# The second head's softmax division in block 1's attention: from VectorE to ScalarE

## The chip, the cores and the metric

The kernel is one program on one core of a Trainium2 chip. The metric is device time in microseconds (us) of one execution. Engines are named as in the profile: PE is TensorE's matmul, PEld its weight load, DVE is VectorE, ACT ScalarE, POOL GpSimd, SP the engine that issues most DMAs.

## What is computed

Two transformer blocks, each of two layers, on 256 tokens (block 1 also on 256 context tokens) with a model width of 1024. The part that matters here is the attention of block 1. It has two branches of eight heads of 64: a neighbourhood attention with a relative bias, and a window attention whose softmax has a sink. Each query looks at its own sequence and at the context:

```python
def sink_softmax(s, sink):
    m = jnp.maximum(jnp.max(s, axis=-1, keepdims=True), sink)
    e = jnp.exp(s - m)
    return e / (jnp.sum(e, axis=-1, keepdims=True) + jnp.exp(sink - m))

s = jnp.concatenate([s_w, s_c], axis=-1)        # scores: own tokens, context
p = jax.nn.softmax(s, axis=-1)                  # neighbourhood; window: sink_softmax
o = p[own] @ v + p[context] @ v_ctx
```

In layer 0 the context tokens are updated too, so they also ask (they look at the context alone); in layer 1 they don't.

## The kernel before

The kernel streams 1 MB chunks of weights through a ring, splits each into a high and a low part (ScalarE line 245, VectorE line 259) and multiplies with three matmuls per product (lines 301 to 303). That takes nearly all of the span. Between two such stretches, in each layer of block 1, stands `attend_both` (line 1738), which runs both branches as one loop of steps with the class `Attention`.

A step is one pair of heads and one tile of 128 queries. The 512 keys (256 own, 256 context) are looked at by tiles of own tokens; tiles of context tokens look at 256 keys. Layer 0 has 32 steps, in which steps of 512 keys and of 256 keys alternate (tiles 0, 2, 1, 3 for each of 8 pairs of heads). Layer 1 has 16 steps, all of 512 keys. Two neighbouring steps of layer 0, the first of 512 keys, are called a pair of steps below.

The order of the work on each engine is written out by hand, one iteration t after the other, and the engines meet through semaphores:

- TensorE: scores of step t (line 808); transposes of the probabilities of step t-2 (`pe_turns`, line 829, eight of 128x128 for 512 keys, four for 256); products with the values of step t-3 (line 843).
- VectorE: adds the bias to both heads' scores of step t and takes the maxima (line 864); reciprocal of the sums of step t-1 (line 873); negated maximum of step t (lines 879, 882); multiplies both heads' probabilities of step t-1 by the reciprocal (line 889); at the end of a pair of heads copies the output (line 902); then in some iterations one or two taps of block 1's convolution (lines 1520, 1524), work that is spread over the loop.
- ScalarE: copies the transposed probabilities of step t-2 from PSUM (`act_turned`, line 914), then the two exponentials of step t, one per head, each with its sum (`act_exp`, line 929).

The waits around the division:

```python
pe.wait_ge(scaled.sem, self.at(scaled, v))                    # line 824, transposes of v
if v:
    pe.wait_ge(turned_sb.sem, self.at(turned_sb, v - 1))      # line 826
dve.wait_ge(small.sem, self.at(small, v))                     # line 886
for half in range(2):                                         # line 887
    p = self.prob[:, v % self.PROBS, half, 0:n]
    o = dve.tensor_scalar(p, p, self.fac[:, v % 3, half:half + 1], ...)
o.then_inc(scaled.sem, 1)
```

`prob` has three buffers, `probT` two, the score banks two. Block 2 uses the same class (lines 2029 and 2039), with an order of its own around it.

Of the kernel before, what the change touches and what calls it, by code (L numbers as in the profile page):

```python
# [23 lines left out]
ACT = mybir.ActivationFunctionType  # L24
# [5 lines left out]
S = 256  # L30
# [87 lines left out]
def build(nc, wstream, xT, ctxT, cT, consts, vecs, rpb, rel, out):  # L118
    ctx = ExitStack()
    with ctx:  # L120
# [8 lines left out]
        def count(name):  # L129
            return Count(ctx.enter_context(nc.semaphore(name)))  # L130
# [594 lines left out]
        small = count("small")  # L725
        floored = count("floored")
        scaled = count("scaled")
        turned = count("turned")
        turned_sb = count("turned_sb")
        summed = count("summed")  # L730
# [3 lines left out]
        class Attention:  # L734
# [7 lines left out]
            LAG_T, LAG_V, PROBS, TURNS = 2, 3, 3, 2  # L742

            def __init__(self, steps, dst, bufs, turn_bank=None, outs=(3072, 3584), halves=False, stacked=False,
                         first_set=0):
                self.stacked, self.first_set = stacked, first_set
                self.steps, self.dst, self.U = steps, dst, len(steps)
                self.turn_bank, self.outs, self.halves = turn_bank, outs, halves
                self.SETS = 1 if turn_bank and not stacked else 2
                self.prob, self.probT, self.mx, self.den, self.fac, self.neg = bufs  # L750
                self.base = {c: c.n for c in (scored, biased, sunk, shift, exped, small, scaled, turned,
                                              turned_sb, summed, taken, taken_hi, floored)}
                self.nsunk = np.cumsum([int("sink" in u) for u in steps]).tolist()
                self.nfloor = np.cumsum([int("floor" in u) for u in steps]).tolist()
                pairs = [u["pair"] for u in steps]
                self.ends = [n for n in range(self.U) if n == self.U - 1 or pairs[n + 1] != pairs[n]]
                for c in (scored, shift, exped, small, scaled, turned, turned_sb, summed):
                    c.n += self.U
                biased.n += 2 * self.U
                sunk.n += self.nsunk[-1]  # L760
                floored.n += self.nfloor[-1]
                taken.n += len(self.ends)
                taken_hi.n += len(self.ends) if halves else 0
                self.length = self.U + self.LAG_V + 1
# [57 lines left out]
            def pe_turns(self, pe, v):  # L822
                if 0 <= v < self.U:
                    pe.wait_ge(scaled.sem, self.at(scaled, v))
                    if v:
                        pe.wait_ge(turned_sb.sem, self.at(turned_sb, v - 1))
                    for half in range(2):
                        for a, w in self.blocks(v):
                            mm = pe.transpose(self.turn(v, half, a)[0:w],  # L829
                                              self.prob[:, v % self.PROBS, half, a:a + w], const("ident"))  # L830
                    mm.then_inc(turned.sem, 1)
# [16 lines left out]
            def dve(self, dve, t):  # L848
                v = t - 1
                if t < self.U:  # L850
                    u = self.steps[t]
                    n = u["n"]
                    slot = t % self.PROBS
                    if t >= self.PROBS:
                        dve.wait_ge(turned.sem, self.at(turned, t - self.PROBS))
                    if "sink" in u:
                        dve.tensor_copy(self.prob[:, slot, :, n:n + 1], u["sink"].unsqueeze(2)).then_inc(sunk.sem, 1)
                    dve.wait_ge(scored.sem, self.at(scored, t))
                    for half in range(2):
                        o, s_in = self.prob[:, slot, half, 0:n], self.score(t, half, n)  # L860
                        if n > 256:
                            o = o.rearrange("p (a k) -> p a k", k=256)
                            s_in = s_in.rearrange("p (a k) -> p a k", k=256)
                        dve.tensor_tensor_reduce(o, s_in, u["bias"][half], 1.0, -3e38, ALU.add, ALU.max,  # L864
                                                 self.mx[:, t % 3, half:half + 1]).then_inc(biased.sem, 1)
                if 0 <= v < self.U:
                    u = self.steps[v]
                    dve.wait_ge(exped.sem, self.at(exped, v))
                    d, f = self.den[:, v % 3, :], self.fac[:, v % 3, :]
                    if "floor" in u:  # L870
                        dve.tensor_scalar(d, d, 1e-30, None, ALU.max).then_inc(floored.sem, 1)
                        dve.wait_ge(floored.sem, self.base[floored] + self.nfloor[v])
                    dve.reciprocal(f, d).then_inc(small.sem, 1)
                if t < self.U:
                    u = self.steps[t]
                    dve.wait_ge(biased.sem, self.base[biased] + 2 * t + 2)
                    m, g = self.mx[:, t % 3, :], self.neg[:, t % 3, :]
                    if "sink" in u:
                        dve.scalar_tensor_tensor(out=g, in0=m, scalar=-1.0, in1=u["minus_sink"], op0=ALU.mult,
                                                 op1=ALU.min).then_inc(shift.sem, 1)  # L880
                    else:
                        dve.tensor_scalar(g, m, u.get("floor", -3e38), -1.0, ALU.max, ALU.mult  # L882
                                          ).then_inc(shift.sem, 1)
                if 0 <= v < self.U:
                    n, gate = self.steps[v]["n"], self.steps[v].get("gate")
                    dve.wait_ge(small.sem, self.at(small, v))
                    for half in range(2):
                        p = self.prob[:, v % self.PROBS, half, 0:n]
                        o = dve.tensor_scalar(p, p, self.fac[:, v % 3, half:half + 1], gate and gate[half], ALU.mult,  # L889
                                              ALU.mult if gate else ALU.bypass)  # L890
                    o.then_inc(scaled.sem, 1)
                v = t - self.LAG_V - int(self.halves)
                if v in self.ends and self.halves:
                    pair = self.steps[v]["pair"]
                    hi, lo = self.dst(pair)
                    dve.wait_ge(taken_hi.sem, self.at(taken_hi, pair))
                    dve.tensor_tensor(lo, self.out(pair)[:, 0:lo.shape[1]], hi.bitcast(F32), ALU.subtract
                                      ).then_inc(taken.sem, 1)
                elif v in self.ends:
                    pair = self.steps[v]["pair"]  # L900
                    dve.wait_ge(summed.sem, self.at(summed, v))
                    dve.tensor_copy(self.dst(pair), self.out(pair)[:, 0:self.dst(pair).shape[1]]
                                    ).then_inc(taken.sem, 1)

            def act_turned(self, act, t):
                v = t - self.LAG_T
                if 0 <= v < self.U:
                    act.wait_ge(turned.sem, self.at(turned, v))
                    if v >= self.TURNS:
                        act.wait_ge(summed.sem, self.at(summed, v - self.TURNS))  # L910
                    bl = self.blocks(v)
                    w, n = bl[-1][1], len(bl) * P
                    at, wide = (self.turn_bank, 512) if self.turn_bank else (2048, 1024)
                    act.activation(self.probT[0:w, v % self.TURNS, :, 0:n],  # L914
                                   psum[0:w, at:at + wide].rearrange("p (h k) -> p h k", h=2)[:, :, 0:n],
                                   ACT.Copy).then_inc(turned_sb.sem, 1)

            def act_exp(self, act, t):
                if t < self.U:
# [818 lines left out]
        def attend_both(layer, tok, conv, nq, nk, nv, na_bias, wq, wk, wv):  # L1738
# [3 lines left out]
            with ExitStack() as st:  # L1742
# [4 lines left out]
                                                             CONSTS["zeros"][0]),  # L1747
                                  (par(layer, "wa_sink"), par(layer, "wa_minus_sink")), 4)
                a = Attention(near + window, lambda pair: (nq, wq)[pair // 4][:, pair % 4, 0:tok],
                              attention_buffers(st, 2 * S), first_set=1)  # L1750
                @block.tensor
                def _(pe):
                    pe.wait_ge(normed.sem, normed.n)
# [14 lines left out]
                @block.scalar  # L1768
                def _(act):
                    for t in range(a.length):  # L1770
                        a.act_turned(act, t)
                        a.act_exp(act, t)


# [1302 lines left out]
```

## Time and profile before

| | us |
|---|---|
| median of 3 runs | 2347.52 (2345.46 to 2348.18) |
| the profiled execution | 2346.48 |
| its span on the core | 2344.7 |
| TensorE busy | 2275.0 (97%), 17296 matmuls |
| VectorE busy | 1498.7 (64%) |
| ScalarE busy | 1190.1 (51%) |
| layer 0's attention (first score to the next stage's first matmul) | 211.77 to 297.59 |
| layer 1's attention | 778.07 to 833.25 |

A span is counted from the first to the last instruction of the core; the time of an execution also holds what lies around it. The share of busy time is an average over the whole kernel; for the attention the windows and timelines of those stretches are read. Matmul records are now and then missing, and a matmul's busy time includes its way through the pipeline, so that starts are a better measure of TensorE than durations.

### The profile page before, as it was taken

How to read it: one execution, taken by the hardware profiler on the slowest of the kernel's cores; microseconds unless marked ns; L12 is line 12 of the kernel's file. 1: busy time of each engine (PE TensorE's matmuls, PEld its weight loads, DVE VectorE, ACT ScalarE, POOL GpSimd, SP SyncE). 2: the span in 40 equal slices, each digit the busy share in tenths (PEclk: the TensorE clock that was granted, in tenths of full speed). 3: DMA queues.
4: the chain of work that ended last, by engine and by line, in shares of the span. 5: the costliest groups of instructions: out<-in, count | busy, mean ns of one | idle time of the engine just before them, and what ended most of it. 6: DMA issues, size and time to landing. Idle time of an engine off the chain costs nothing.

```text
span 2344.7 us, 44800 instructions
## 1 busy us (share of the span) xinstructions
PE 2275.0 (97%) x17296; PEld 2053.5 (88%) x17296; DVE 1498.7 (64%) x2663; ACT 1190.1 (51%) x1934; POOL 244.3 (10%) x272
## 2 busy tenths in 40 slices
PE   7999999999999999999999999999999998999998
PEld 4777677788878699999989899999999988999998
DVE  6487974453468865655486766654665677667654
ACT  6344743643355656534366564543544565555443
POOL 1012000000012000022010100221131001000320
PEclk9999999999999999999999999999999999999999
DMA  8321034344233035645554335455455454344552
GB/s 306 112 99 55 2 110 159 144 167 142 87 124 120 35 126 181 215 179 192 196 183 161 123 129 196 162 194 195 151 194 197 164 191 140 131 159 163 195 197 90
DMA packets 61842, 355.59 MB, mean 152 GB/s; under 512 B 6208, under 2 KB 19712, under 8 KB 20352
## 3 DMA queue, kind: packets, MB, share of 16 engines
q1 hardware_dynamic: 61552, 353.55, 42.2%
q8 instruction: 102, 1.67, 0.3%
q14 instruction: 44, 0.36, 0.0%
q10 hardware_dynamic: 144, 0.01, 0.0%
HBM read 349.29 MB, written 1.10 MB: 149 GB/s over the span
## 4 chain that ended last, share of the span: by engine, by line
PE 86%; DVE 9%; ACT 3%; issue 1%; DMA 1%; POOL 0%; ACTq 0%; SPq 0%; DVEq 0%
PE psum L301 20%; PE psum L303 20%; PE psum L302 20%; PE psum L1908 3%; PE psum L1909 3%; PE psum L1906 3%; PE psum L829 2%; DVE w_lo L259 2%; PE psum L843 2%; PE psum L808 2%; DVE prob L889 1%; DVE prob L864 1%; DVE conv_out L1524 1%; PE psum L658 1%; PE psum L379 1%
## 5 line engine op out<-in xcount | busy, mean ns | idle before, releaser
L259 DVE TENSOR_TENSOR w_lo<-ring,w_hi 128x1024 fp32r<-128x1024 f32 x638 | 813.2, 1307 | 434.9 <-ACT w_hi L245 434.5
L301 PE MATMUL psum<-halves,w_hi 128*128 128x256 f32 (+1 forms) x3314 | 1002.9, 303 | 15.2 <-DVE halves L608 6.7
L303 PE MATMUL psum<-halves,w_lo 128*128 128x256 f32 (+1 forms) x3314 | 985.0, 297 | 0.0
L302 PE MATMUL psum<-halves,w_hi 128*128 128x256 f32 (+1 forms) x3314 | 984.4, 297 | 0.0
L245 ACT ACTIVATE w_hi<-ring 128x1024 fp32r<-128x1024 f32 (+1 forms) x638 | 644.0, 1049 | 294.5 <-PE psum L303 138.1
L301 PEld LDWEIGHTS psum<-halves,w_hi 128*128 128x128 f32 x3314 | 623.9, 188 | 51.0 <-issue 13.1
L302 PEld LDWEIGHTS psum<-halves,w_hi 128*128 128x128 f32 x3314 | 624.1, 188 | 25.7 <-issue 1.7
L303 PEld LDWEIGHTS psum<-halves,w_lo 128*128 128x128 f32 x3314 | 623.4, 188 | 23.2
L1906 PE MATMUL psum<-h_hi,w_hi 128*128 (+1 forms) x640 | 176.6, 276 | 0.0
L1908 PE MATMUL psum<-h_lo,w_hi 128*128 (+1 forms) x640 | 176.6, 276 | 0.0
L1909 PE MATMUL psum<-h_hi,w_lo 128*128 (+1 forms) x640 | 176.6, 276 | 0.0
L1930 ACT ACTIVATE gate<-psum 128x256 f32<-128x256 f32 x88 | 33.9, 385 | 258.3 <-PE psum L303 258.3
L914 ACT ACTIVATE probT<-psum 128x512 f32<-128x512 f32 (+3 forms) x128 | 79.5, 621 | 151.1 <-PE psum L829 151.1
L1981 POOL CAST h_hi<-hid 128x256 f32 (+1 forms) x88 | 35.1, 399 | 989.1 <-DVE hid L1950 989.1
L929 ACT ACTIVATE prob<-prob,neg 128x256 f32<-128x256 f32 (+6 forms) x256 | 127.6, 502 | 14.1 <-DVE neg L882 13.5
L1906 PEld LDWEIGHTS psum<-h_hi,w_hi 128*128 128x128 f32 x640 | 120.1, 188 | 0.0
L1908 PEld LDWEIGHTS psum<-h_lo,w_hi 128*128 128x128 f32 x640 | 120.1, 188 | 0.0
L1909 PEld LDWEIGHTS psum<-h_hi,w_lo 128*128 128x128 f32 x640 | 120.1, 188 | 0.0
L1950 DVE SCALAR_TENSOR_TENSOR hid<-psum,gate 128x256 f32<-128x256 f32 x88 | 37.4, 425 | 125.6 <-ACT gate L1930 125.6
L1983 POOL TENSOR_TENSOR h_lo<-hid,h_hi 128x256 f32 (+1 forms) x88 | 111.1, 1262 | 13.5 <-POOL h_hi L1981 12.7
L1524 DVE SCALAR_TENSOR_TENSOR conv_out<-cpad,vec,conv_out 128x512 f32<-128x512 f32 (+1 forms) x180 | 107.7, 664 | 0.0
L829 PEld LDWEIGHTS psum<-cst,prob 128*128 128x128 f32 (+1 forms) x544 | 58.7, 140 | 48.3 <-DVE prob L889 38.3
(334 smaller groups left out, 2927.2 us busy)
## 6 DMA issues: line engine op xcount, KB each, us to landing
ring<-wstream SPq DMA_DIRECT2D x320, 1024.0 KB, 4.8
x<-xT SPq DMA_DIRECT2D x2, 1024.0 KB, 7.6
x<-ctxT SPq DMA_DIRECT2D x2, 1024.0 KB, 10.0
rel_bias<-bias_by_distance SPq DMA_DIRECT2D x2, 1024.0 KB, 9.0
fox_bias<-forgetting_sums SPq DMA_DIRECT2D x2, 1024.0 KB, 8.1
cst<-consts SPq DMA_DIRECT2D x1, 1534.0 KB, 11.9
wk<-wk_once SPq DMA_DIRECT2D x8, 128.0 KB, 4.2
kk_sw<-kk_sw SPq DMA_DIRECT2D x8, 128.0 KB, 5.8
```

The costliest lines, as they stand in the source:

```text
L245: act.activation(w_hi[:, c % 2, h], ring[:, (c + 2 * i) % RING, h], ACT.Copy).then_inc(hi_done.sem, 1)
L259: dve.tensor_tensor(w_lo[:, c % 2, h], ring[:, (c + 2 * i) % RING, h], w_hi[:, c % 2, h].bitcast(F32), ALU.subtract).then_inc(split_done.s ...
L301: pe.matmul(o, w_hi[:, c, w_cols], hi, start=first, stop=False)
L302: pe.matmul(o, w_hi[:, c, w_cols], lo, start=False, stop=False)
L303: return pe.matmul(o, w_lo[:, c, w_cols], hi, start=False, stop=last)
L829: mm = pe.transpose(self.turn(v, half, a)[0:w], self.prob[:, v % self.PROBS, half, a:a + w], const("ident"))
L929: o = act.activation(p, p, ACT.Exp, bias=self.neg[:, t % 3, half:half + 1], accum_out=self.den[:, t % 3, half:half + 1])
L1524: dve.scalar_tensor_tensor(out=o, in0=src, scalar=wc, in1=o, op0=ALU.mult, op1=ALU.add).then_inc(conv_step.sem, 1)
L1906: pe.matmul(o, w_hi[:, c, b:b + P], h_hi[:, kt, :], start=start and k == 0, stop=False)
L1908: pe.matmul(o, w_hi[:, c, b:b + P], h_lo[:, kt, :], start=False, stop=False)
L1909: mm = pe.matmul(o, w_lo[:, c, b:b + P], h_hi[:, kt, :], start=False, stop=False)
L1983: pool.tensor_tensor(h_lo[:, j, :], hid[:, s, :], h_hi[:, j, :].bitcast(F32), ALU.subtract).then_inc(lower.sem, 1)
```

## The change

In block 1's attention alone (`shared=True`), VectorE multiplies only the first head's probabilities of a step, and ScalarE the second head's, with a copy whose scale is the reciprocal, read from SBUF. In ScalarE's order the new instruction of step t-1 stands between the copy of the transposes of step t-2 and the exponentials of step t. TensorE waits for both engines before it transposes. Block 2 is not touched.

```diff
             def pe_turns(self, pe, v):
                 if 0 <= v < self.U:
                     pe.wait_ge(scaled.sem, self.at(scaled, v))
+                    if self.shared:
+                        pe.wait_ge(scaled_second.sem, self.f0 + v + 1)
                     if v:
                         pe.wait_ge(turned_sb.sem, self.at(turned_sb, v - 1))
...
                     dve.wait_ge(small.sem, self.at(small, v))
-                    for half in range(2):
+                    for half in range(1 if self.shared else 2):
                         p = self.prob[:, v % self.PROBS, half, 0:n]
...
+            def act_scale(self, act, v):
+
+                if self.shared and 0 <= v < self.U:
+                    act.wait_ge(small.sem, self.at(small, v))
+                    p = self.prob[:, v % self.PROBS, 1, 0:self.steps[v]["n"]]
+                    act.activation(p, p, ACT.Copy, scale=self.fac[:, v % 3, 1:2]).then_inc(scaled_second.sem, 1)
...
                     for t in range(a.length):
                         a.act_turned(act, t)
+                        a.act_scale(act, t - 1)
                         a.act_exp(act, t)
```

ScalarE in layer 0, two iterations from t = 3 on (an odd step of 256 keys, then an even one of 512). `probT` is the copy of the transposes, `prob` the probabilities, `den` the sums, `fac` the reciprocals, `neg` the negated maxima. Before:

```order
L914 ACTIVATE probT<-psum 128x2x256 [waits turned]
L929 ACTIVATE prob,den<-prob,neg 128x256 [waits small,shift]
L929 ACTIVATE prob,den<-prob,neg 128x256
L914 ACTIVATE probT<-psum 128x1024 [waits summed,turned]
L929 ACTIVATE prob,den<-prob,neg 128x512 [waits small,shift]
L929 ACTIVATE prob,den<-prob,neg 128x512
```

The same with the change (its line numbers are shifted: 919 is line 914 of before, 941 is 929, and 928 is new):

```order
L919 ACTIVATE probT<-psum 128x2x256 [waits turned]
L928 ACTIVATE prob<-prob,fac 128x512 [waits small]
L941 ACTIVATE prob,den<-prob,neg 128x256 [waits small,shift]
L941 ACTIVATE prob,den<-prob,neg 128x256
L919 ACTIVATE probT<-psum 128x1024 [waits summed,turned]
L928 ACTIVATE prob<-prob,fac 128x256 [waits small]
L941 ACTIVATE prob,den<-prob,neg 128x512 [waits small,shift]
L941 ACTIVATE prob,den<-prob,neg 128x512
```

Between the copy of a step's transposes and the next exponentials there is now the multiply of the step after it. No load of an activation table stands inside either loop.

TensorE in layer 0 at the same place. Before:

```order
L808 MATMUL psum<-nk,nq 128x256 [waits biased]
L808 MATMUL psum<-nk,nq 128x256
L829 MATMUL psum<-cst,prob 128x128 [waits turned_sb,scaled]
L829 MATMUL psum<-cst,prob 128x128 x3
L843 MATMUL psum<-probT,nv 64x128 [waits turned_sb]
```

With the change (811, 834 and 848 are lines 808, 829 and 843):

```order
L811 MATMUL psum<-nk,nq 128x256 [waits biased]
L811 MATMUL psum<-nk,nq 128x256
L834 MATMUL psum<-cst,prob 128x128 [waits turned_sb,scaled_second,scaled]
L834 MATMUL psum<-cst,prob 128x128 x3
L848 MATMUL psum<-probT,nv 64x128 [waits turned_sb]
```

The order of the matmuls is as it was; the first transpose of each step waits for one semaphore more, which ScalarE raises.

## Rows read from the trace of the kernel before

**Rows 1.** The chain that ended last: shares of the span by engine, whole kernel

```profile
PE 86%; DVE 9%; ACT 3%; issue 1%; DMA 1%; POOL 0%; ACTq 0%; SPq 0%; DVEq 0%
```

**Rows 2.** Windows A:B: length, busy us (count) of PE, PEld, DVE, ACT, POOL; granted clock, DMA share

```profile
222.02:297.59 75.57, 73.37 (x662) 47.03 (x660) 65.71 (x261) 58.35 (x148) 0.00 (x0) 1.00 0.01 2
789.24:833.25 44.01, 42.65 (x403) 28.39 (x401) 40.34 (x138) 34.05 (x69) 0.00 (x0) 1.00 0.01 1
```

**Rows 3.** Waits of layer 0's attention, 211 to 298 us: total us, times, longest

```profile
PEld psum L829 <- DVE prob L889: 20.5, 30, 2.6
ACT probT L914 <- PE psum L829: 18.2, 17, 1.8
...
PE psum L829 <- DVE prob L889: 3.2, 6, 1.7
```

**Rows 4.** Timeline, one pair of layer 0: start, us, engine, line [idle before <- releaser]

```profile
228.08 1.09 PE L829 MATMUL psum<-cst,prob 128*128 128x128 f32 x8
...
229.21 1.02 ACT L914 ACTIVATE probT<-psum 128x1024 f32<-128x1024 f32 x1 [1.10 <-PE psum L829]
...
229.73 0.62 DVE L889 TENSOR_SCALAR prob<-prob,fac 128x256 f32<-128x256 f32 x2
...
230.13 0.71 ACT L929 ACTIVATE prob<-prob,neg 128x512 f32<-128x512 f32 x1
...
230.40 0.42 PEld L829 LDWEIGHTS psum<-cst,prob 128*128 128x128 f32 x4 [0.41 <-DVE prob L889]
...
231.54 0.58 ACT L914 ACTIVATE probT<-psum 128x512 f32<-128x512 f32 x1
231.67 0.17 DVE L873 RECIPROCAL fac<-den 128x2 f32<-128x2 f32 x1
...
233.08 1.09 PE L829 MATMUL psum<-cst,prob 128*128 128x128 f32 x8
```

**Rows 5.** Timeline: three score starts on TensorE in layer 0

```profile
222.02 1.13 PE L808 MATMUL psum<-nk,nq 64*128 64x512 f32 x4
...
282.54 0.30 PEld L808 LDWEIGHTS psum<-wk,wq 64*128 64x128 f32 x4 [0.17 <-issue]
...
287.48 1.13 PE L808 MATMUL psum<-wk,wq 64*128 64x512 f32 x4
```

**Rows 6.** Groups by form, VectorE, 211 to 298 us: busy us, mean ns

```profile
L889 DVE TENSOR_SCALAR prob<-prob,fac 128x512 f32<-128x512 f32 x32 | 14.1, 484 | 0.0
...
L889 DVE TENSOR_SCALAR prob<-prob,fac 128x256 f32<-128x256 f32 x32 | 9.9, 352 | 0.0
```

**Rows 7.** Groups by form, ScalarE, whole kernel: busy us, mean ns

```profile
L700 ACT ACTIVATE x<-x,vec 128x256 f32<-128x256 f32 x40 | 16.5, 495 | 0.0
...
L1188 ACT ACTIVATE conv_out<-conv_out,vec 128x256 f32<-128x256 f32 x4 | 2.1, 590 | 0.0
...
L1180 ACT ACTIVATE prod<-conv_out 128x256 f32<-128x256 f32 x4 | 1.3, 408 | 0.0
```

**Rows 8.** Timeline, the end of layer 0's attention

```profile
294.41 1.02 ACT L914 ACTIVATE probT<-psum 128x1024 f32<-128x1024 f32 x1 [0.83 <-PE psum L829]
295.55 0.42 PEld L829 LDWEIGHTS psum<-cst,prob 128*128 128x128 f32 x4 [0.83 <-issue]
```

**Rows 9.** Timeline, one step of layer 1

```profile
790.30 1.09 PE L829 MATMUL psum<-cst,prob 128*128 128x128 f32 x8
...
791.43 1.03 ACT L914 ACTIVATE probT<-psum 128x1024 f32<-128x1024 f32 x1 [0.68 <-PE psum L829]
...
794.54 1.03 ACT L914 ACTIVATE probT<-psum 128x1024 f32<-128x1024 f32 x1 [0.68 <-PE psum L829]
```

**Rows 10.** Timeline, the end of layer 1's attention

```profile
820.31 1.13 PE L808 MATMUL psum<-wk,wq 64*128 64x512 f32 x4
...
823.57 1.13 PE L808 MATMUL psum<-wk,wq 64*128 64x512 f32 x4
...
830.01 0.86 PEld L829 LDWEIGHTS psum<-cst,prob 128*128 128x128 f32 x8 [0.40 <-DVE prob L889]
```

More of the change, by code:

```diff
@@ L727, in build @@
         scaled = count("scaled")
+        scaled_second = count("scaled_second")
         turned = count("turned")
@@ L744, in __init__ @@
             def __init__(self, steps, dst, bufs, turn_bank=None, outs=(3072, 3584), halves=False, stacked=False,
-                         first_set=0):
-                self.stacked, self.first_set = stacked, first_set
+                         first_set=0, shared=False):
+                self.stacked, self.first_set, self.shared = stacked, first_set, shared
                 self.steps, self.dst, self.U = steps, dst, len(steps)
@@ L758, in __init__ @@
                     c.n += self.U
+                self.f0 = scaled_second.n
+                scaled_second.n += self.U if shared else 0
                 biased.n += 2 * self.U
@@ L1749, in attend_both @@
                 a = Attention(near + window, lambda pair: (nq, wq)[pair // 4][:, pair % 4, 0:tok],
-                              attention_buffers(st, 2 * S), first_set=1)
+                              attention_buffers(st, 2 * S), first_set=1, shared=True)
                 @block.tensor
```

## Prediction

> **What bounds the kernel now.** The chain that ended last comes first: 86% of it is TensorE's [rows 1], so time on another engine counts only where TensorE waits for it. The change touches two stretches, so I read the windows of those [rows 2]. In both TensorE is busy nearly throughout (73.37 of 75.57 us in layer 0, 42.65 of 44.01 in layer 1), at a granted clock of 1.00; VectorE has 65.71 and 40.34 us of work, ScalarE 58.35 and 34.05. So VectorE is fuller than ScalarE in both, which is what a shift of work would use; but neither is the bound. The waits of layer 0 say how little VectorE delays TensorE: weight loads stand idle 20.5 us "for" the division, but those loads run ahead of the matmuls, and the matmuls themselves wait 3.2 us in 6 places [rows 3], most of it at the loop's start, before it is full. In the same view ScalarE waits 18.2 us for transposes. That row matters most here: ScalarE starts each copy of transposes the moment TensorE has made them, so whatever is put behind that copy starts late, however idle ScalarE is on average.
>
> The pace is read from starts. Layer 0: scores of 512 keys at 222.02 and, 13 pairs of steps later, at 287.48 [rows 5], so 65.46 / 13 = 5.035 us a pair; the quickest pair, 282.54 to 287.48 in the same rows, takes 4.94, which is about what TensorE needs with no wait at all. Layer 1: 791.43 to 794.54, 3.11 us a step [rows 9].
>
> **The edits.** VectorE loses one multiply a step: 0.484 us at 512 keys, 0.352 at 256 [rows 6]. ScalarE gains one multiply of the same shape. Before has no ScalarE copy with a scale from SBUF. Nearest are instructions whose bias is read from SBUF: the exponential of 512 columns, 0.71 us [rows 4], and L700 of 256, 0.495 [rows 7]. Bounds at 256 columns are 0.408 us (nothing read beside the data, L1180) and 0.590 (scale and bias both read, L1188) in the same group as L700. I take 0.495 and 0.71: one operand is read. The next ScalarE instruction can start some 0.09 us before the recorded end: a copy of 1.02 us at 229.21 is followed at 230.13, so by 0.92 [rows 4].
>
> **Layer 0, the loop that decides.** Count from the start P of a step's eight transposes, 228.08 in [rows 4]. ScalarE's copy starts at 229.21, P+1.13, and gives ScalarE free at 230.13, P+2.05. Before, the exponentials start there, and TensorE's next transposes (256 keys) start at 230.40, P+2.32, behind their own queue of values and scores; the multiplies they need are VectorE's and end at 229.73+0.62 = 230.35, just 0.05 before. After, the second head's multiply of these 256 keys can't start before P+2.05, ends at P+2.05+0.495 = P+2.545, and TensorE sees it about 0.12 later: the handover from ScalarE to a transpose shows at the end of layer 0, where a copy ends at 294.41+1.02 = 295.43 and the transposes start at 295.55 [rows 8]. So P+2.665 in place of P+2.32. From there TensorE needs 233.08-230.40 = 2.68 us to the next eight transposes [rows 4], 2.67 where nothing waits. A pair then takes 2.665+2.67 = **5.335** us, 0.30 more than 5.035. TensorE stands idle about 0.35 us a pair, just ahead of the short transposes.
>
> Do the other loops fit in 5.335? The exponentials of 512 keys start at P+2.05+0.40 = P+2.45, take the 1.41 us from 230.13 to the next copy at 231.54, so end P+3.86; copy of 256, 0.48: P+4.34; multiply of 512: P+4.34+0.71+0.12 = P+5.17, before the P+5.335 at which TensorE wants it. The reciprocal it needs follows the exponentials by about 0.13 (231.54 to 231.67 in the same rows), so at P+4.2: in time. The 256-key exponentials then end at about P+5.9, and the next copy starts at P+6.47. So only the first loop binds. VectorE's taps, its output copies and its sink copies keep their places and get more slack.
>
> 14 pairs (the 13 counted, and the one ahead of them, where the copy of step 0 likewise has to end first) at 0.30: +4.2 us. The drain of the loop has no scores for TensorE to do meanwhile. Counting again from the last long-key transposes but one, P = 287.48+1.06 = 288.54: transposes 30 at P+5.17, their copy P+5.17+1.13+0.92 = P+7.22, the last multiply and handover +0.495+0.12 = P+7.84. Before they start at 295.55, P+7.01 [rows 8]. So another +0.8. Layer 0: **+5.0 us**.
>
> **Layer 1.** The same loop with 512 keys only: 1.13+0.92+0.71+0.12 = 2.88 us from transposes to transposes, against TensorE's own 3.11. From [rows 9]: transposes 790.30, copy 791.43, next copy 794.54. ScalarE's load is 0.92+0.62+1.41 = 2.95 of 3.11. TensorE stays the bound. VectorE's relief gives back what it costs late in the loop: 820.31 to 823.57 is 3.26 instead of 3.11 [rows 10], 0.15, and about 0.1 at the start, where one multiply ends sooner on ScalarE than two on VectorE. In the drain, score 823.31: transposes 824.37, copy 825.50 to 826.42, multiply and handover 827.25, but ScalarE is in the last exponentials until 828.45; copy to 829.37, last multiply 830.20, against 830.01 in [rows 10]. Layer 1: **+0.2 us**: what is gained in the loop is lost in the drain.
>
> **One rule against one row.** VectorE's multiply takes 0.352 us at 256 keys, ScalarE's instruction of that size 0.495 [rows 6, 7]. The Trainium skill (ScalarE: Activation LUTs, Rules for kernel authors) says to keep multiplications on VectorE; by that rule alone each moved instruction costs its difference, which is the third case below. The trace agrees on the direction of the price.
>
> **The sum.** Before's profiled execution took 2346.48 us; +5.0+0.2 gives 2351.7. The median of the runs is 1.04 above that execution, so I forecast **2352.7**, 0.22% slower. Some 0.2%, 4.7 us, is what a measurement of this kernel can tell from no change, so the forecast lies just beyond that edge. Terms at their bounds: a handover of 0.06 (VectorE's at 230.40 took about 0.05) takes 0.06 x 16, so 1.0 us off; a multiply of 0.408 another 0.087 x 15 = 1.3; one of 0.590 adds 1.4. That is +2.9 to +6.6.
>
> **Rivals.**
> - *TensorE stays the bound everywhere and only VectorE's waits go.* Then a pair falls to 4.94: 13 x 0.095 = 1.2 us less, and 0.3 less in layer 1: 2346.0. For it: ScalarE is idle 1.1 us ahead of each long copy [rows 4] and VectorE is the fuller engine [rows 2]. Against: the idle time lies before the copy and the multiply stands behind it. It decides if the multiply can be seen by P+2.27, so if it takes under about 0.2 us; no row of ScalarE is that short at 256 columns. Chance 0.1. It is not slower.
> - *ScalarE binds layer 1 too.* Slack there is 3.11-2.95 = 0.16 us a step. With a multiply of 0.90 instead of 0.71 (two operands, 0.804, and another 0.1 for waits ahead of it) 16 steps lose about 0.05 each and layer 0's pairs another 0.2: 5.2+0.8+2.8 = +8.8, 2356.3. For it: three instructions with a wait each follow one another on ScalarE now. Against: copy and exponential before follow without a gap [rows 4]. Chance 0.08.
> - *The full price of the move.* If each moved instruction costs its difference, 32 x (0.71-0.484) + 16 x (0.495-0.352) = 9.5 us, 2357.0. Against: in layer 1 neither duration is on the path. Chance 0.04. The rule of the Trainium skill's page ScalarE: Activation LUTs would come out so.
> - *The forecast*, with its bounds: 0.78. About 0.28 of that lies under +4.7.
>
> Slower by over 0.2%: 0.50+0.08+0.04 = 0.62. Within 0.2%: 0.28 and nearly all of the first rival, 0.36. Faster: 0.02. The range leaves out the first rival and most of the last two: from +2.9 less 1.4 us for the spread of the runs, to +6.6 with 1.6 for spread and part of the second: 2349.0 to 2355.7.
>
> **What would show it.** In layer 0, scores of 512 keys every 5.3 us, TensorE's short transposes waiting some 0.35 us for ScalarE's new line and its first long exponential 0.40 us later behind the copy; layer 0's attention some 5 us longer. In layer 1, 3.11 us a step throughout, the 3.26 gone, and no idle time of TensorE between the start and the drain. The new instruction 0.49 and 0.71 us. The forecast is wrong if pairs of layer 0 keep under 5.1 us, if layer 1's steps grow, or if time moves outside the two loops.

## The result, and the profile after

| | before | change |
|---|---|---|
| median of 15 runs each, us | 2347.28 (2345.46 to 2349.67) | 2350.70 (2349.07 to 2353.0) |
| ratio | | 1.0015, interval 1.0008 to 1.0022 |
| profiled execution, us | 2346.48 | 2351.58 |
| span, us | 2344.7 | 2349.8 |
| layer 0's attention, us | 85.82 | 89.18 |
| layer 1's attention, us | 55.18 | 54.48 |

The change costs 3.4 us, 0.15%, with an interval of 1.9 to 5.2 us. That is inside the range, short of the forecast 5.2 and within 0.2%, while I held "slower by over 0.2%" to be likelier. The prediction took 0.2% for what a measurement can tell from no change; this one tells 0.15%. In this profile the two loops together are 2.66 us longer; the rest of the 5.1 us between the two spans lies outside them, where the kernels do the same (more on this under why the prediction was right).

Ratios compare ordinary executions: one of before at 2392 us and two of the kernel with the short steps only at 7951 and 9307 us, which nothing here explains, are left out of them.

The chain that ended last hardly moves: VectorE had 9% of it [rows 1].

```profile
PE 87%; DVE 7%; ACT 4%; issue 1%; DMA 1%; POOL 0%; ACTq 0%; SPq 0%; DVEq 0%
```

Windows of the steady part of both loops; after the length come the busy times (counts) of PE, PEld, DVE, ACT and POOL, the granted clock, DMA's share and GB/s:

```profile
222.33:301.97 79.64, 73.11 (x662) 47.04 (x661) 56.84 (x231) 73.26 (x178) 0.00 (x0) 1.00 0.01 1
792.38:836.60 44.22, 42.55 (x402) 28.40 (x400) 36.03 (x124) 42.30 (x83) 0.00 (x0) 1.00 0.01 1
```

Against [rows 2] the work has moved as the diff says. In layer 0 VectorE falls from 65.71 to 56.84 us and ScalarE rises from 58.35 to 73.26, now 92% of its window. TensorE does the same 662 matmuls (73.11 us busy, 73.37 before) in a window that is 4.1 us longer. Layer 1's window holds the same work of TensorE in 44.22 us, against 44.01.

Waits of layer 0 (total us, times, longest), to be read beside [rows 3]:

```profile
PEld psum L834 <- DVE prob L894: 24.1, 30, 2.5
...
PE psum L834 <- ACT prob L928: 9.1, 18, 1.7
...
ACT probT L919 <- PE psum L834: 6.6, 17, 0.8
```

The third row is the sign to look for: ScalarE's waits for transposes fell from 18.2 to 6.6 us because ScalarE now does something in that time, and in exchange TensorE's matmuls wait 9.1 us for the new multiply (second row; 1.7 of it is the loop's start, where TensorE waited as long before, for VectorE). The first row grew too, from 20.5 to 24.1, and names VectorE, which had long finished: it is a weight load that ran ahead and waits for several semaphores. This row alone would send a reader to the wrong engine.

One pair of steps in layer 0, as in [rows 4]. Line 834 is the transposes, 919 the copy, 928 the new multiply, 941 the exponentials, 894 VectorE's multiply:

```profile
228.69 1.09 PE L834 MATMUL psum<-cst,prob 128*128 128x128 f32 x8
...
229.82 1.02 ACT L919 ACTIVATE probT<-psum 128x1024 f32<-128x1024 f32 x1 [0.39 <-PE psum L834]
...
230.34 0.35 DVE L894 TENSOR_SCALAR prob<-prob,fac 128x256 f32<-128x256 f32 x1
...
230.74 0.50 ACT L928 ACTIVATE prob<-prob,fac 128x256 f32<-128x256 f32 x1
231.13 0.71 ACT L941 ACTIVATE prob<-prob,neg 128x512 f32<-128x512 f32 x1
...
231.31 0.42 PEld L834 LDWEIGHTS psum<-cst,prob 128*128 128x128 f32 x4 [0.71 <-DVE prob L894]
231.34 0.63 PE L834 MATMUL psum<-cst,prob 128*128 128x128 f32 x4 [0.34 <-ACT prob L928]
...
232.55 0.58 ACT L919 ACTIVATE probT<-psum 128x512 f32<-128x512 f32 x1
...
233.02 0.72 ACT L928 ACTIVATE prob<-prob,fac 128x512 f32<-128x512 f32 x1
...
233.97 0.14 PEld L834 LDWEIGHTS psum<-cst,prob 128*128 128x128 f32 x1 [0.76 <-DVE prob L894]
```

From the eight transposes at P = 228.69: copy P+1.13, multiply P+2.05, its end P+2.55, transposes P+2.62, where the forecast had P+2.665. TensorE idles 0.34 us there (231.34), VectorE's half of the job having ended at 230.69. The long exponentials start at P+2.44 (forecast P+2.45). The next eight transposes come at 233.97, 5.29 us after the last (counting the weight loads of both, 228.68 and 233.97).

The new instruction, ScalarE by form (busy us, mean ns):

```profile
L928 ACT ACTIVATE prob<-prob,fac 128x512 f32<-128x512 f32 x32 | 22.9, 715 | 0.5 <-DVE fac L878 0.5
...
L928 ACT ACTIVATE prob<-prob,fac 128x256 f32<-128x256 f32 x16 | 8.0, 500 | 0.0
```

0.500 and 0.715 us, against 0.495 and 0.71 assumed from [rows 4, 7].

The end of layer 0, against [rows 8]:

```profile
299.35 0.50 ACT L928 ACTIVATE prob<-prob,fac 128x256 f32<-128x256 f32 x1
299.92 0.42 PEld L834 LDWEIGHTS psum<-cst,prob 128*128 128x128 f32 x4 [1.18 <-issue]
```

Here 299.35+0.50 = 299.85, and the transposes' loads start at 299.92: a handover of 0.07 us, where [rows 8] had shown 0.12.

Layer 1, one step, against [rows 9]:

```profile
793.43 1.09 PE L834 MATMUL psum<-cst,prob 128*128 128x128 f32 x8
...
794.57 1.02 ACT L919 ACTIVATE probT<-psum 128x1024 f32<-128x1024 f32 x1
...
795.49 0.71 ACT L928 ACTIVATE prob<-prob,fac 128x512 f32<-128x512 f32 x1
```

The copy runs from 794.57 and the multiply follows without a gap at 795.49. The next transposes are at 796.54, 3.11 us after the last, as before. The start of the last scores and of the last transposes, against [rows 10]:

```profile
826.55 1.13 PE L811 MATMUL psum<-wk,wq 64*128 64x512 f32 x4
...
830.44 0.85 PEld L834 LDWEIGHTS psum<-cst,prob 128*128 128x128 f32 x8 [0.96 <-DVE prob L894]
...
833.37 0.86 PEld L834 LDWEIGHTS psum<-cst,prob 128*128 128x128 f32 x8 [1.05 <-DVE prob L894]
833.40 1.06 PE L834 MATMUL psum<-cst,prob 128*128 128x128 f32 x8 [0.84 <-ACT prob L928]
```

From the last scores to the last transposes 6.82 us, against 830.01-823.57 = 6.44 before: the drain pays 0.38 us.

### The profile page after: what moved, and what is told of

It reads as the page before. It is cut to its first block, busy times and chain, and to the rows that moved or that the text cites. A ratio compares the mean times of both kernels' runs of the same rounds, so it can differ in the third digit from the quotient of the medians.

```text
span 2349.8 us, 44802 instructions
## 1 busy us (share of the span) xinstructions
PE 2273.9 (97%) x17296; PEld 2055.1 (87%) x17296; DVE 1482.9 (63%) x2615; ACT 1215.0 (52%) x1982; POOL 245.2 (10%) x272
## 4 chain that ended last, share of the span: by engine, by line
PE 87%; DVE 7%; ACT 4%; issue 1%; DMA 1%; POOL 0%; ACTq 0%; SPq 0%; DVEq 0%
PE psum L301 20%; PE psum L303 20%; PE psum L302 20%; PE psum L1919 3%; PE psum L1922 3%; PE psum L1921 3%; PE psum L834 3%; PE psum L848 3%; DVE w_lo L259 2%; PE psum L811 2%; PE psum L658 1%; PE psum L379 1%; PE psum L380 1%; PE psum L369 1%; PE psum L368 1%
```

## The experiments

Edits are against the change where nothing else is said. All times of loops count from the first score to the next stage's first matmul, and "pair" is the mean of 13 pairs of steps of layer 0, from the fifth score on. The clock is the mean from the first to the fifth score of layer 0 and of layer 1. Ratios are from 10 or 11 executions of a kernel, with two exceptions: 4 of the multiply before the copy, 5 of the short multiply in two pieces; before ran again beside each group (22 to 29 executions). Rows without a ratio are single executions.

| kernel | ratio to before (interval) | pair, us | layer 0, us | layer 1, us | clock at the two starts |
|---|---|---|---|---|---|
| before | | 5.04 | 85.82 | 55.18 | 0.83, 0.85 |
| before, profiled again | | 5.04 | 84.94 | 54.46 | 1.00, 1.00 |
| the change | 1.0015 (1.0008 to 1.0022) | 5.29 | 89.18 | 54.48 | 1.00, 1.00 |
| long steps only | 0.9996 (0.9987 to 1.0005) | 4.98 | 84.07 | 55.32 | 1.00, 0.85 |
| short steps only | 1.0019 (1.0010 to 1.0028) | 5.29 | 90.17 | 54.44 | 0.84, 1.00 |
| multiply before copy | 1.0061 (1.0045 to 1.0076) | 5.79 | 96.55 | 58.12 | 1.00, 1.00 |
| short multiply in two pieces | 1.0030 (1.0017 to 1.0043) | 5.47 | 92.11 | 54.48 | 1.00, 1.00 |
| half the columns | 1.0006 (0.9997 to 1.0015) | 5.18 | 87.47 | 55.31 | 1.00, 0.85 |
| before, matmuls in the first wait | 0.9996 (0.9988 to 1.0005) | 5.04 | 84.94 | 54.46 | 1.00, 1.00 |
| the change, matmuls in the first wait | 1.0016 (1.0007 to 1.0025) | 5.29 | 89.19 | 54.48 | 1.00, 1.00 |
| long steps, matmuls | | 4.98 | 84.03 | 54.48 | 1.00, 1.00 |
| long steps but the last two, matmuls | 0.9984 (0.9975 to 0.9993) | 4.98 | 84.04 | 53.72 | 1.00, 1.00 |
| the same again | 0.9989 (0.9980 to 0.9998) | 4.98 | 84.05 | 53.73 | 1.00, 1.00 |
| the same without matmuls | 0.9991 (0.9982 to 1.0000) | 4.98 | 84.92 | 53.72 | 0.83, 1.00 |

**Before, profiled once more.** No edit.

> The kernel before, unchanged, profiled once more. In its first profile TensorE's granted clock at the start of both attention loops was 0.83 and 0.85, in the changed kernel's it was 1.00, which made the first four steps 0.7 and 0.9 us shorter there. Theory A (the order of work at the start decides the clock): again the low clock, first score to fifth score 10.2 us in layer 0 and 11.1 in layer 1. Theory B (the low clock comes and goes from one execution to the next): this profile can show 1.00, and then 9.5 and 10.3 us, the same as in the changed kernel. Pairs of steps in layer 0: 5.03 us in both theories.

Windows from the first to the fifth score of both loops (columns as above), in the profile that the prediction read, and in the new one:

```profile
211.77:222.02 10.25, 7.75 (x45) 4.33 (x44) 6.33 (x28) 6.47 (x16) 0.00 (x0) 0.83 0.03 14
778.07:789.24 11.17, 9.14 (x49) 4.49 (x48) 9.38 (x33) 7.41 (x15) 0.00 (x0) 0.85 0.00 0
```

```profile
212.59:221.89 9.30, 6.27 (x45) 3.33 (x45) 6.25 (x28) 6.39 (x15) 0.00 (x0) 1.00 0.04 16
777.74:788.21 10.47, 7.59 (x50) 3.77 (x49) 9.26 (x32) 7.53 (x15) 0.00 (x0) 1.00 0.00 0
```

The same windows of the change:

```profile
212.79:222.33 9.54, 6.24 (x45) 3.33 (x44) 5.63 (x26) 7.34 (x17) 0.00 (x0) 1.00 0.04 16
782.12:792.38 10.26, 7.54 (x50) 3.78 (x49) 8.66 (x31) 8.32 (x17) 0.00 (x0) 1.00 0.00 1
```

Theory B: the same program, the same order of work, another clock. With the low clock the four steps took 10.25 and 11.17 us, without it 9.30 and 10.47. At equal clock the change costs 89.18-84.94 = 4.24 us in layer 0 and 54.48-54.46 = 0.02 in layer 1: 4.3 us, well inside the measured interval. The 0.7 us that the change seems to gain in layer 1 was a difference of clocks.

**Long steps only.** ScalarE multiplies only steps of 512 keys.

```diff
+                self.on_act = [shared and u["n"] == 512 for u in steps]
+                self.nact = np.cumsum([int(a) for a in self.on_act]).tolist()
...
-                    if self.shared:
-                        pe.wait_ge(scaled_second.sem, self.f0 + v + 1)
+                    if self.on_act[v]:
+                        pe.wait_ge(scaled_second.sem, self.f0 + self.nact[v])
...
-                    for half in range(1 if self.shared else 2):
+                    for half in range(1 if self.on_act[v] else 2):
...
-                if self.shared and 0 <= v < self.U:
+                if 0 <= v < self.U and self.on_act[v]:
```

> ScalarE multiplies the second head only of steps with 512 keys; with 256 keys VectorE does both again. Theory (the round trip over the short multiply binds layer 0): the pair falls from 5.29 us to TensorE's own 4.95 to 5.0, a little under before's 5.035, and layer 1 stays as in the change, so the kernel takes before's time or up to 1.5 us less: ratio to before 0.9993 to 1.0000. Rival (it is ScalarE's added load, or the third semaphore of TensorE's wait, that costs): 16 of 32 multiplies of layer 0 and 0.71 of each 1.21 us of added load remain, so pairs of 5.18 us and a ratio of about 1.001.

Its timeline (836 transposes, 921 copy, 943 exponentials):

```profile
250.50 0.85 PEld L836 LDWEIGHTS psum<-cst,prob 128*128 128x128 f32 x8 [0.76 <-DVE prob L896]
...
251.63 1.02 ACT L921 ACTIVATE probT<-psum 128x1024 f32<-128x1024 f32 x1 [0.43 <-PE psum L836]
...
252.55 0.71 ACT L943 ACTIVATE prob<-prob,neg 128x512 f32<-128x512 f32 x1
...
252.82 0.42 PEld L836 LDWEIGHTS psum<-cst,prob 128*128 128x128 f32 x4 [0.41 <-DVE prob L896]
```

After the copy the long exponentials follow at once (252.55), and the short transposes start 2.32 us after the long ones, as in [rows 4]. The pair takes 4.98 us, less than before's 5.04. 0.72 us of multiply a pair is still on ScalarE, and the long transposes still wait for the third semaphore; neither costs anything. The rival's 5.18 is excluded.

**Short steps only.** The same edit with `== 256`.

> ScalarE multiplies the second head only of steps with 256 keys; with 512 keys VectorE does both. Layer 1 is then exactly before's. Theory (round trip over the short multiply): the pair stays at 5.27 to 5.30 us, the whole loss of layer 0 stays, ratio to before 1.0015 to 1.002. Rival (added load): only 0.50 of 1.21 us a pair remains, pairs of 5.14 us, ratio about 1.0006.

```profile
230.12 0.86 PEld L836 LDWEIGHTS psum<-cst,prob 128*128 128x128 f32 x8 [0.76 <-DVE prob L896]
...
232.18 0.50 ACT L930 ACTIVATE prob<-prob,fac 128x256 f32<-128x256 f32 x1
...
232.74 0.42 PEld L836 LDWEIGHTS psum<-cst,prob 128*128 128x128 f32 x4 [0.71 <-DVE prob L896]
...
235.41 0.85 PEld L836 LDWEIGHTS psum<-cst,prob 128*128 128x128 f32 x8 [0.76 <-DVE prob L896]
```

The multiply (line 930) ends at 232.68, the short transposes start 0.06 later, 2.62 us after the long ones, and the pair is 5.29 us: the change's, to the hundredth. One instruction of 0.50 us a pair carries the whole loss of layer 0. Kernel time 1.0019, against 1.0015 of the change; the intervals overlap.

**The multiply ahead of the copy.**

```diff
-                        a.act_turned(act, t)
                         a.act_scale(act, t - 1)
+                        a.act_turned(act, t)
                         a.act_exp(act, t)
```

> The change, with ScalarE's multiply put ahead of the copy of the transposes in each iteration instead of behind it. Same instructions on every engine, another order. Theory (what counts is the loop an instruction closes, not its load): the multiply of 256 keys comes 0.4 us sooner, but now the copy stands behind a wait for VectorE's reciprocal, which itself follows ScalarE's exponentials. One turn of layer 0 on ScalarE is then 0.92 (copy) + 1.51 (long exponentials and their sum) + 0.24 (reciprocal and its handovers) + 0.62 (multiply) + 0.48 + 1.08 + 0.24 + 0.40 for the short step = 5.5 us at least, up to 5.8 where VectorE's reciprocal comes behind its bias work; layer 1: 0.92 + 1.51 + 0.24 + 0.62 = 3.3 us a step in place of 3.11. In all 6 to 11 us slower than the change, ratio to before 1.004 to 1.006. Rival (load): pairs 5.29 and steps 3.11 as in the change, ratio 1.0018.

```profile
230.53 0.19 ACT L941 ACTIVATION_READ_ACCUMULATOR prob<-prob,neg 128x1 f32 x1
...
231.14 0.16 DVE L878 RECIPROCAL fac<-den 128x2 f32<-128x2 f32 x1
...
231.33 0.51 ACT L928 ACTIVATE prob<-prob,fac 128x256 f32<-128x256 f32 x1 [0.61 <-DVE fac L878]
...
231.75 1.00 ACT L919 ACTIVATE probT<-psum 128x1024 f32<-128x1024 f32 x1
...
232.87 0.41 PEld L834 LDWEIGHTS psum<-cst,prob 128*128 128x128 f32 x4 [1.10 <-issue]
232.90 0.63 PE L834 MATMUL psum<-cst,prob 128*128 128x128 f32 x4 [0.72 <-ACT probT L919]
```

The short exponentials' sum comes at 230.72, the reciprocal only at 231.14, behind VectorE's bias work; then the multiply at 231.33 (its engine idle 0.6 us), and the copy, whose transposes were ready, at 231.75. The short transposes now wait for that copy, to 232.90, because the transposes of all steps are written to one place in PSUM (`turn`), which the copy has to empty first (the wait of line 826 of before). The pair takes 5.79 us, a step of layer 1 takes (43.63-10.89)/10 = 3.27. Same instructions, with loops 11 us longer than the change's, the upper end of what was expected: load explains none of it.

**Length of the short multiply.** Longer, by cutting it in two instructions:

```diff
-                    p = self.prob[:, v % self.PROBS, 1, 0:self.steps[v]["n"]]
-                    act.activation(p, p, ACT.Copy, scale=self.fac[:, v % 3, 1:2]).then_inc(scaled_second.sem, 1)
+                    n = self.steps[v]["n"]
+                    cuts = (0, n // 2, n) if n == 256 else (0, n)
+                    for a, b in zip(cuts, cuts[1:]):
+                        p = self.prob[:, v % self.PROBS, 1, a:b]
+                        o = act.activation(p, p, ACT.Copy, scale=self.fac[:, v % 3, 1:2])
+                    o.then_inc(scaled_second.sem, 1)
```

> The change, with ScalarE's multiply of 256 keys cut in two of 128 columns, one behind the other. The first costs about 0.30 us before the next can start, the second 0.39 to its end, so 0.69 in place of 0.50. Theory (the round trip binds, and each us of the short multiply is a us of the pair): pair 5.29 + 0.19 = 5.48 us, 14 pairs and the drain, 2.9 us slower than the change, ratio to before 1.0030. Layer 1 unchanged. Rival (TensorE's own work binds, with some fixed cost of the handover): pair 5.29, ratio 1.0018.

```profile
230.41 0.68 ACT L931 ACTIVATE prob<-prob,fac 128x128 f32<-128x128 f32 x2
...
231.16 0.42 PEld L834 LDWEIGHTS psum<-cst,prob 128*128 128x128 f32 x4 [0.89 <-DVE prob L894]
```

Shorter, by leaving the lower 128 columns to VectorE:

```diff
-                    for half in range(1 if self.shared else 2):
-                        p = self.prob[:, v % self.PROBS, half, 0:n]
+                    for half in range(1 if self.shared and n == 512 else 2):
+                        p = self.prob[:, v % self.PROBS, half, 0:(n // 2 if self.shared and half else n)]
...
-                    p = self.prob[:, v % self.PROBS, 1, 0:self.steps[v]["n"]]
+                    n = self.steps[v]["n"]
+                    p = self.prob[:, v % self.PROBS, 1, (n // 2 if n == 256 else 0):n]
```

> The change, with ScalarE taking only the upper 128 of the 256 columns of a short step's second head, VectorE the lower 128. 512 keys as in the change. Theory (round trip): ScalarE's short multiply 0.39 us in place of 0.50, pair 5.29 - 0.11 = 5.18 us, 1.7 us faster than the change, ratio to before about 1.0011. Rival (fixed cost): pair 5.29. VectorE's added 0.25 us a pair is hidden in both.

```profile
230.51 0.39 ACT L929 ACTIVATE prob<-prob,fac 128x128 f32<-128x128 f32 x1
...
230.97 0.42 PEld L834 LDWEIGHTS psum<-cst,prob 128*128 128x128 f32 x4 [0.60 <-DVE prob L894]
```

Multiplies of 0.39, 0.50 and 0.68 us give pairs of 5.18, 5.29 and 5.47: each 0.1 us of it is 0.1 us of the pair. Read backwards, and this is an estimate, the pair would reach 4.98, where it no longer binds, with a multiply of about 0.19 us.

**The start's clock.** Before, and the change, each with seven matmuls on constants in TensorE's wait for the first multiply; their output goes to the place of the transposes in PSUM, which is written next.

```diff
-                        a.pe(pe, t)
+                        a.pe_score(pe, t)
+                        if t == 2:
+                            keep_awake(pe, 7, 2048)
+                        a.pe_rest(pe, t)
```

> The kernel before, with seven matmuls on constants (their output goes to a bank that is overwritten next) put into TensorE's wait ahead of the first transposes of each loop. Theory A (idle time of TensorE at the start lowers its clock): the granted clock at the start is 1.00 in both layers, first to fifth score 9.5 and 10.3 us, and the kernel 1.0 to 1.6 us faster than before. Theory B (the low clock falls at random): no difference of the medians, ratio 1.0000. The seven matmuls take about 2 us and end about when the multiplies do; if they end later, 0.2 us is lost in each layer.

> The change, with the seven constant matmuls in TensorE's wait at the start of each loop. Of 16 loop starts profiled so far without them 5 had a granted clock of 0.83 to 0.85, of 4 with them none. Theory A (idle time of TensorE there lets the clock fall in some executions, and matmuls prevent it): both starts at 1.00, 9.5 and 10.3 us to the fifth score; ratio to before about 1.0015, as 5 of 16 starts at 0.8 us each is only 0.25 us a loop. Theory B (chance alone): each start has some 3 in 10 of the low clock.

Both kernels have all their starts at clock 1.00, and the loops of before profiled again and of the change, unchanged. The medians can't resolve it: 0.9996 and 1.0016, with intervals that hold 1.0000 and the change's own 1.0015. Over all profiles, 6 of 18 starts without the matmuls had the low clock, and none of 10 with them; at 12 in 18 for a good start, ten in a row by chance would be 2 in 100, and if the six low starts are dealt out at random among all 28, they miss these ten in 5 of 100 cases. So the matmuls likely prevent it, which isn't shown; if they do, it is worth about a third of 0.7 to 0.9 us a loop (an estimate).

**Long steps but the last two, and the matmuls.** ScalarE multiplies the long steps but for the last two of each loop, where the drain had paid, and the seven matmuls stand in TensorE's first wait.

```diff
+                self.on_act = [shared and u["n"] == 512 and n < len(steps) - 2 for n, u in enumerate(steps)]
```

> ScalarE multiplies the second head of steps with 512 keys but for the last two steps of each loop, where VectorE does both, and seven constant matmuls stand in TensorE's wait at the start. Theory: pairs of layer 0 at 4.94 to 5.07 us as with the long steps alone, first to fifth score 9.2 us at a granted clock of 1.00, layer 1 3.11 us a step, and its drain back from 10.05 to 9.5 to 9.7 us. Layer 0 then takes 84.0 us and layer 1 54.0, against 84.9 and 54.5 of before at the same clock: 1.3 us less, ratio 0.9990 to 1.0000. Rival (the drain is set by the last exponentials alone): layer 1 stays at 54.4.

The rest of the edit is as in the two sections above. The last transposes of layer 1:

```profile
825.28 0.86 PEld L836 LDWEIGHTS psum<-cst,prob 128*128 128x128 f32 x8 [0.86 <-DVE prob L896]
...
827.55 0.85 PEld L836 LDWEIGHTS psum<-cst,prob 128*128 128x128 f32 x8 [0.39 <-DVE prob L896]
```

The matmuls of the last transposes but one, in this version and in before's second profile:

```profile
825.29 1.09 PE L836 MATMUL psum<-cst,prob 128*128 128x128 f32 x8 [0.62 <-DVE prob L896]
```

```profile
826.69 1.09 PE L829 MATMUL psum<-cst,prob 128*128 128x128 f32 x8 [0.99 <-DVE prob L889]
```

The last transposes start at 827.55, 2.27 us after those before them; in the change the distance was 833.37-830.44 = 2.93. The drain is back at 9.30 us from 10.05 and even below before's 9.68, since TensorE waits 0.62 us for the second last multiply and not 0.99: VectorE, which had less to do until then, comes to it sooner. The loops save 0.90+0.74 = 1.6 us of before's at equal clock; 3.7 us of kernel time were more than that. Three more kernels asked which was right: the same without the seven matmuls, the same again, and the long steps with the matmuls and with the last two on ScalarE.

> Long steps but the last two on ScalarE, without the seven matmuls. The same with them was measured at 0.9984 [0.9975, 0.9993] of before, 3.7 us less, where the two loops are only 1.6 us shorter at the same clock. If the order of work carries it, this kernel takes 1.6 us less than before, ratio 0.9993, and the rest of the 3.7 us is the clock and scatter; if the seven matmuls carry more than their 0.5 us, this kernel is at 0.9993 and the next again at 0.9984.

> The kernel that was fastest so far, once more: long steps but the last two on ScalarE and the seven matmuls. Expected by its loops 1.6 us less than before, and 0.5 us for the clock: 0.9991. If 0.9984 was right, it comes again. Both starts at clock 1.00 by theory A.

> Long steps alone on ScalarE, with the seven matmuls: layer 0 84.0 us, layer 1 54.5 us from first score to the next stage, clock 1.00 at both starts by theory A, 3 in 10 of a low one at each by theory B.

The loops repeat to 0.01 us; without the matmuls layer 0 once more fell into the low clock. The ratios, 0.9984, 0.9989 and without matmuls 0.9991, have intervals that overlap, and those of the last two hold the 0.9993 that the loops alone give. So this version is faster than before by 0.1% or a little less, the 0.9984 was probably in part scatter, and what the matmuls add is too small to be told from these medians. With the last two steps on ScalarE layer 1 took 54.48 us: the rival, that the last exponentials alone set the drain, falls.

## Why the prediction was right, and where it was off

- *TensorE bounds both loops, and time counts only where it waits.* Right: halving VectorE's multiply of the long steps moved little by itself; the pair went from 5.04 to 4.98 with the long steps alone, the 0.06 that VectorE's waits had cost on average (0.095 was forecast against the quickest pair).
- *The round trip transposes, copy, multiply, transposes is layer 0's bound.* Right, and shown four ways: by taking the short multiply away (4.98), by leaving it alone (5.29), by two other lengths of it (5.18, 5.47). The forecast P+2.665 was P+2.62. One reading on the way was too broad: not each copy of transposes starts the moment TensorE has made them, only those of the long steps do, and the last of the loop. The copy at 231.54 in [rows 4] follows the exponentials with no wait, and the 17 waits in [rows 3] are about half of the 32 copies. The loop that binds goes through the long copy, so nothing of the sum hung on it.
- *The term that was mis-sized.* The handover: I took 0.12 us from the one place where a transpose waited for ScalarE [rows 8]; it was 0.07 here. In the layer 0 loop that is 0.05 in 14 pairs and twice in the drain, 0.8 us. With it: pairs 5.335 - 0.05 = 5.285, measured 5.29, so +0.25 a pair in place of +0.30. This was inside the bounds given. The one waits for the copy's semaphore, the other for the multiply's, and that it isn't scatter the kernel with the multiply ahead of the copy shows: there too a copy ends at 232.75 and the weight loads start at 232.87, 0.12 later. Why the two differ stays open.
- *The start.* I gave the first pair 0.30 us like the others. At equal clock it was 9.54-9.30 = 0.24. The profile of before had a low clock there, so its loops were 0.9 and 0.7 us longer than those of its second profile. It would have misled me by 1.6 us, had the sum been made against its windows rather than by differences.
- *The drain.* Forecast +0.8 in layer 0, measured 0.74 (8.18 against 7.44 us from the last scores).
- *Layer 1 +0.2.* Measured 0.02: start -0.21 (forecast -0.1), the steps until the fifteenth score 31.06 us in both, then the 0.15 us of VectorE's late slip gone, drain +0.37 (0.45). The mechanism held, one gain was twice as large.
- *Sum.* 3.26 in 13 pairs, 0.24 at the start, 0.74 in the drain, 0.02 in layer 1: 4.3 us at equal clock, for 5.2 forecast. The 15 runs say 3.4, the 11 runs of the change with the matmuls 4.0 (2350.81 against 2346.80).
- *Time outside the loops* was named as a sign that the forecast is wrong, and the first profiles show it: the change takes 1.0 us more ahead of layer 0's attention, 0.3 less between the two and 1.8 more after layer 1's. It is most likely scatter. After layer 1's attention the change took 1513.2 us and before 1511.4; the long steps but the last two with the matmuls took 1512.7 and, the same kernel again, 1510.6, and the change with its short multiply in two pieces 1511.4.
- *The rivals.* None came. Layer 1 kept 3.11 us a step, so ScalarE's slack of 0.16 us was enough. The price by durations, 9.5 us, was far off: the rule of the Trainium skill (ScalarE: Activation LUTs, Rules for kernel authors) gives the sign for the short steps, where each extra 0.1 us counts in full, though not the reason: by that slope even a multiply of VectorE's 0.35 us would, in this place, make pairs of about 5.14 us (an estimate), against before's 5.04. It doesn't give the sign for the long ones, where 0.72 us on ScalarE in place of 0.49 on VectorE costs nothing in the loop.
- *The chances.* With the loop's pairs as sure as they were, the doubt lay in whether the sum passes 4.7 us; a handover from VectorE had shown 0.05 in [rows 4], and the middle of the two would have put the forecast at 4.6 and the larger chance on "within 0.2%".

## What to carry to other kernels

An engine's idle share is no room for new work; room is the time between the last thing an instruction needs and the moment its result is wanted, and here the idle time of ScalarE lay ahead of the copy while the multiply had to stand behind it. Walk one turn of the loop from starts, through the instruction that is put in and back to the engine that bounds, for each size of step by itself: the long steps had 0.2 us of slack, the short ones were 0.3 short. Where the answer differs by size or place in the loop, move the work only where there is slack, and mind the drain, in which the bounding engine has nothing else to do.

## What the runs showed of the hardware

- TensorE's granted clock at the loop start, where TensorE waits 1.7 us for the first multiply, was 0.83 to 0.85 in 6 of 18 starts and 1.00 in the others, with the same program (before) at both. The mean hides two levels: eight transposes took 1.97 us at 217.19 of the first profile, at 1.2 GHz, and 1.09 later, at 2.4 GHz. The Trainium skill (TensorE: Matmul & The Clock Gate, Part 1: The HAM clock gate) says of the spell at the low clock at a kernel's start that it varies from run to run with the same kernel; these profiles show the same in mid-kernel. In none of 10 starts with matmuls put into the wait was the clock low.
- The idle time of 0.34 us that TensorE has in every pair of the change did not lower its clock: 1.00 through layer 0.
- ScalarE's copy with a scale read from SBUF takes 0.39, 0.50 and 0.715 us at 128, 256 and 512 columns, in place, and the next instruction starts 0.1 us before its end.
